# A hybrid attention and HGRN2 block: the second weight pair as four blocks instead of seven products

## The reference

```
proj = h @ w_in                       # (1024, 1024) @ (1024, 10240)
sb_q, sb_k, sb_v, sb_z, hg_q, hg_f, hg_i, hg_z, gate_logits = split(proj)
w[i, j] = sigmoid(z_ij) * prod_{j < l < i} (1 - sigmoid(z_il)),  z = q k^T / sqrt(128)   # stick-breaking, 8 heads
f = lb + (1 - lb) sigmoid(hg_f);  S_t = f S_{t-1} + (1 - f) v_t^T;  o_t = S_t^T silu(hg_q)   # HGRN2, 8 heads
y = sigmoid(gates_sb) * (sb_o * silu(sb_z)) @ w_sb + sigmoid(gates_hg) * (norm(hg_o) * silu(hg_z)) @ w_hg
out = rmsnorm(x + y @ w_out) * final_norm_g
```

## Time and profile before

| what | us |
|---|---|
| median of 3 runs | 1380.04 (1379.36 to 1381.21) |
| the profiled execution | 1382.87 |
| its span | 1381.1 |
| TensorE busy | 1340.9 (97%) |
| VectorE busy | 944.4 (68%) |
| GpSimd busy | 724.6 (52%) |
| ScalarE busy | 585.0 (42%) |

### The profile page before, as it was taken

The page is one execution under the profiler, slowest core; times in us unless marked ns, Lnnn a source line. Parts: engine busy times, 40 slices in busy tenths (PEclk is TensorE's granted clock), DMA queues, the critical chain, the costliest instruction groups (busy, mean ns, idle before and its releaser), DMA issues.

```text
span 1381.1 us, 23094 instructions
## 1 busy us (share of the span) xinstructions
PE 1340.9 (97%) x8421; PEld 1115.3 (81%) x8421; DVE 944.4 (68%) x1075; ACT 585.0 (42%) x965; POOL 724.6 (52%) x484
## 2 busy tenths in 40 slices
PE   7989999999999999999999999999999989999998
PEld 6778788788888878878878888887877868788886
DVE  5868877877967987787796797888544634545323
ACT  7645356256346435625634633653444411101121
POOL 5965554744665556565466456554678622223210
PEclk9989999999999999999999999999999999999999
DMA  5111311121112211121111211115452475433502
GB/s 184 31 46 31 93 61 32 63 77 46 63 31 67 63 56 61 32 90 64 31 63 59 64 63 32 62 40 145 167 192 98 143 238 191 134 92 122 199 26 103
DMA packets 128221, 119.41 MB, mean 86 GB/s; under 512 B 3920, under 2 KB 110464, under 8 KB 128128
## 3 DMA queue, kind: packets, MB, share of 16 engines
q1 hardware_dynamic: 118912, 92.84, 21.2%
q10 hardware_dynamic: 9216, 25.17, 5.2%
HBM read 88.63 MB, written 29.36 MB: 85 GB/s over the span
## 4 chain that ended last, share of the span: by engine, by line
PE 83%; DVE 5%; POOL 3%; issue 2%; ACT 1%; DMA 1%; DVEq 0%; ACTq 0%; POOLq 0%
PE banks L1695 46%; PE banks L2005 11%; PE banks L2027 6%; PE banks L1780 5%; PE banks L1756 4%; PE banks L1770 2%; POOL b_lo L638 1%; PE banks L1839 1%; POOL b_sum L638 1%; DVE hk L1176 1%; PE banks L1814 1%; PE banks L1739 1%; PE banks L1841 1%; PE banks L1834 1%; PE banks L1820 1%
## 5 line engine op out<-in xcount | busy, mean ns | idle before, releaser
L1695 PE MATMUL banks<-a_hi,b_hi 128*128 128x512 f32 x1092 | 444.5, 407 | 9.0 <-DVE k_raw L1176 4.3
L1695 PE MATMUL banks<-a_hi,b_lo 128*128 128x512 f32 x1092 | 428.5, 392 | 0.0
L1695 PE MATMUL banks<-a_lo,b_hi 128*128 128x512 f32 x1092 | 427.4, 391 | 0.0
L638 POOL TENSOR_TENSOR b_lo<-w_raw,b_hi 128x512 fp32r<-128x512 f32 x106 | 162.2, 1540 | 222.6 <-ACT b_hi L747 222.6
L638 POOL TENSOR_TENSOR b_lo<-b_sum,b_hi 128x512 fp32r<-128x512 f32 x117 | 176.0, 1504 | 156.0 <-ACT b_hi L747 156.0
L1695 PEld LDWEIGHTS banks<-a_hi,b_hi 128*128 128x128 f32 x1092 | 205.9, 189 | 51.3 <-issue 6.8
L1695 PEld LDWEIGHTS banks<-a_hi,b_lo 128*128 128x128 f32 x1092 | 205.7, 188 | 45.5
L1695 PEld LDWEIGHTS banks<-a_lo,b_hi 128*128 128x128 f32 x1092 | 206.4, 189 | 37.1
L1307 DVE TENSOR_TENSOR_SCAN kappa<-kappa 128x128 f32<-128x128 f32 (+3 forms) x64 | 90.9, 1421 | 86.6 <-ACT kappa L924 86.6
L747 ACT ACTIVATE b_hi<-b_sum 128x512 fp32r<-128x512 f32 x117 | 73.9, 632 | 156.1 <-POOL b_sum L638 151.2
L731 POOL TENSOR_TENSOR w_lo<-w_raw,w_hi 128x1024 fp32r<-128x1024 f32 x20 | 54.9, 2747 | 143.8 <-ACT w_hi L747 143.8
(11 more groups left out here) (218 smaller groups left out, 2584.5 us busy)
## 6 DMA issues: line engine op xcount, KB each, us to landing
w_raw<-in_w_in SPq DMA_DIRECT2D x72, 512.0 KB, 5.0
gate_d<-gate_out SPq DMA_DIRECT2D x16, 512.0 KB, 3.3
gate_in<-gate_d ACTq DMA_DIRECT2D x32, 256.0 KB, 2.7
x_tok<-in_x SPq DMA_DIRECT2D x8, 512.0 KB, 5.7
z_d<-z_out SPq DMA_DIRECT2D x8, 512.0 KB, 2.6
hz_d<-z_out SPq DMA_DIRECT2D x8, 512.0 KB, 2.6
osb_d<-o_sb SPq DMA_DIRECT2D x8, 512.0 KB, 7.1
ohg_d<-hq SPq DMA_DIRECT2D x8, 512.0 KB, 2.7
```

The lines of the kernel that those rows point to most:

```text
L638: return nc.gpsimd.tensor_tensor(dst, a, b, op)
L1695: last = mm(bank, w[:, s, k, :], t[s][:, k, :], start=opens and k == 0 and z == 0, stop=k == QUAD - 1 and z == 2, skip_group_check=not opens)
```

## The change

The second pair is done like the first, in four blocks of (token half, panel): (1, 0), (1, 1), (0, 0), (0, 1), into banks 4 to 7. Its weights are split without sums, in places named by `second_weights`, one of them the first pair's. GpSimd makes four low halves in place of seven and three sums. ScalarE copies the finished blocks to `turn_in` and `z_out` (`take_second`), between the splits of the third pair; VectorE's sums over them are gone, and so are `c12_step` and its wait. VectorE makes the low halves of k and q before those of P5 and P3. The high half of P3 now waits for two blocks of the second pair. TensorE waits for `block_taken` 5 and for all four sums of h (`s_ready` 4) after the second pair. SyncE loads the third pair after the second's last low half. `sum_t7` of the third pair raises `raw_sum` by 9, so that later counts agree. The small rows are fetched by ScalarE's queue ahead of `norm_tiles`. `fetch_gate(0)` stands before the last `finish_gate` and its waits.

```diff
-SECOND_ORDER = (P1, P2, P4, P7, P6, P5, P3)
-SECOND_BANKS = {P1: 4, P2: 5, P4: 6, P7: 7, P6: 2, P5: 4, P3: 3}
+SECOND_BLOCKS = {(1, 0): 4, (1, 1): 5, (0, 0): 6, (0, 1): 7}
+FIRST_SUM = 9
...
     if isinstance(n, int) and n == 1:
-        return PRODUCTS + SECOND_ORDER.index(s) + 1
+        return {P2: PRODUCTS + 3, P3: PRODUCTS + 3, P4: 2 * PRODUCTS, P6: PRODUCTS}.get(s, 1)
...
+        def second_weights(rows, panel):
+            s = {(0, 0): P2, (1, 0): P3, (0, 1): P4}.get((rows, panel))
+            return first_b[0, 0] if s is None else (b_hi[:, s, :, :], b_lo[:, s, :, :])
...
@@ sync, load_pair and the first loads @@
                 elif isinstance(n, int) and n == 2:
-                    sp.wait_ge(raw_sum, 4 * n)
-                    sp.wait_ge(w_ready, PRODUCTS + SECOND_SPLIT_ORDER.index(P3) + 1)
+                    sp.wait_ge(w_ready, 2 * PRODUCTS)
...
             load_x(1)
-            load_small(0, KT, norm_g[0].rearrange("(k p) -> k p", p=P))
...
             load_x(2)
@@ gpsimd @@
             pool.wait_ge(w_loaded, 32)
-            second_split(P1, raw_block(0, 0))
-            second_split(P2, raw_block(1, 0))
-            tt(part_of(b_sum, P5), raw_block(0, 1), raw_block(0, 0), ALU.subtract).then_inc(raw_sum, 5)
...
+            for i, (rows, panel) in enumerate(FIRST_BLOCKS[:3]):
+                second_low(rows, panel, i + 1)
             pool.wait_ge(a_ready, KT)
             tt(flat(raw_a12), flat(a_hi[P2]).bitcast(F32), flat(a_lo[P2]).bitcast(F32), ALU.add).then_inc(a_back, 1)
-            second_split(P4, part_of(b_sum, P4))
-            second_split(P7, part_of(b_sum, P7))
             pool.wait_ge(first_rows_done, 1)
-            second_split(P6, t2_flat)
-            second_split(P5, part_of(b_sum, P5))
+            second_low(*FIRST_BLOCKS[3], 4)
@@ scalar @@
+            load_small(0, KT, norm_g[0].rearrange("(k p) -> k p", p=P))
...
             norm_tiles(0, 4)
...
             sum_high(P7, raw_s3, s3_made)
-            split_second(P4)
+            split_second(3)
             sum_high(P6, raw_s2, s2_made)
-            for s in (P7, P6, P5):
-                split_second(s)
             sum_high(P5, raw_s1, s1_made)
             take_first(1, 3)
             take_first(3, PRODUCTS)
-            sum_high(P3, raw_s4, s4_made)
-            act.wait_ge(product_done, products_before(1, P1))
-            copy(u3[:, :], banks[:, SECOND_BANKS[P1], :]).then_inc(p1_copied, 2)
...
             copy(k_hi[:, :], first_out[:, 2:4, :].rearrange("p a n -> p (a n)")).then_inc(k_hi_ready, 1)
-            split(2, SPLIT_ORDER[0])
             copy(q_hi[:, :], first_out[:, 0:2, :].rearrange("p a n -> p (a n)")).then_inc(q_hi_ready, 1)
+            for t in SPLIT_ORDER[:2]:
+                split(2, t)
...
+            def take_second(tokens, panel, done):
+                act.wait_ge(product_done, PRODUCTS + done)
+                return copy(halfs((turn_in, z_out)[panel], tokens), banks[:, SECOND_BLOCKS[tokens, panel], :])
+            take_second(1, 0, 1).then_inc(p1_copied, 2)
+            act.wait_ge(qk_split, 2)
+            take_second(1, 1, 2).then_inc(block_taken, 5)
+            sum_high(P3, raw_s4, s4_made)
             act.wait_ge(lb_step, 1)
             nc.scalar.activation(lb[:, :], lb_low, ACT.Sigmoid).then_inc(lb_step, 1)
-            for t in SPLIT_ORDER[2:-1]:
+            for t in SPLIT_ORDER[2:4]:
                 split(2, t)
+            take_second(0, 0, 3).then_inc(first_taken, 2)
+            for t in SPLIT_ORDER[4:-1]:
+                split(2, t)
+            take_second(0, 1, PRODUCTS).then_inc(block_taken, 5)
...
-            finish_gate(N_GATE_PAIRS - 1)
-            for i in range(2):
-                act.wait_ge(gate_stored[i], 16 * N_GATE_PAIRS)
+            fetch_gate(0)
+            finish_gate(N_GATE_PAIRS - 1)
+            for i in range(2):
+                act.wait_ge(gate_stored[i], 16 * N_GATE_PAIRS)
             act.wait_ge(product_done, PRODUCTS * N_PAIRS)
             fetch_ohg(0)
-            fetch_gate(0)
             fetch_ohg(1)
@@ vector @@
             low_sum(P6, raw_s2, 2)
+            dve.wait_ge(k_hi_ready, 1)
+            tt(k_lo[:, :], first_out[:, 2:4, :]..., k_hi[:, :].bitcast(F32), ALU.subtract).then_inc(qk_split, 1)
+            dve.wait_ge(q_hi_ready, 1)
+            tt(q_lo[:, :], first_out[:, 0:2, :]..., q_hi[:, :].bitcast(F32), ALU.subtract).then_inc(qk_split, 1)
             low_sum(P5, raw_s1, 3)
             low_sum(P3, raw_s4, 4)
...
-            second_done(P2)
-            tt(halfs(turn_in, 0), second_bank(P2), u3[:, :], ALU.add).then_inc(first_taken, 1)
...
-            tt(u2[:, :], second_bank(P5), u2[:, :], ALU.add).then_inc(c12_step, 1)
...
@@ tensor @@
-                    if isinstance(h, int) and h == 0:
-                        pe.wait_ge(c12_step, 1)
...
-            for s in SECOND_ORDER:
-                second_product(s)
+            for i, ((tokens, panel), bank) in enumerate(SECOND_BLOCKS.items()):
+                if i == 0:
+                    pe.wait_ge(w_ready, PRODUCTS + 2)
+                    pe.wait_ge(s3_made, QUAD)
+                if i == 1:
+                    pe.wait_ge(w_ready, 2 * PRODUCTS)
+                if i == 2:
+                    pe.wait_ge(s1_made, QUAD)
+                for k in range(KT):
+                    last = first_block(tokens, panel, k, second_weights, bank)
+                last.then_inc(product_done, 1 if i < 3 else 4)
+            pe.wait_ge(block_taken, 5)
+            pe.wait_ge(s_ready, 4)
             pe.wait_ge(const_made, CONSTANTS)
```

More of the change, by code:

```diff
@@ L646, in sum_t7 @@
             def sum_t7(n, raw=w_raw):
-                tt(part_of(b_sum, P7), raw_block(0, 1, raw), raw_block(1, 1, raw), ALU.subtract).then_inc(raw_sum, 1)
+                tt(part_of(b_sum, P7), raw_block(0, 1, raw), raw_block(1, 1, raw), ALU.subtract).then_inc(
+                    raw_sum, FIRST_SUM if isinstance(n, int) and n == 2 else 1)
             def sum_t5(n, raw=w_raw):
@@ L677, in _, with second_low @@
                 tt(raw_a11[:, k, :], a_hi[P1][:, k, :].bitcast(F32), a_lo[P1][:, k, :].bitcast(F32), ALU.add).then_inc(a_back, 1)
-            def second_split(s, raw):
-                split(1, SECOND_SPLIT_ORDER, s, raw)
-            pool.wait_ge(w_loaded, 32)
-            second_split(P1, raw_block(0, 0))
-            second_split(P2, raw_block(1, 0))
-            tt(part_of(b_sum, P5), raw_block(0, 1), raw_block(0, 0), ALU.subtract).then_inc(raw_sum, 5)
[L687 to L692, removed]
+            def second_low(rows, panel, made):
+                pool.wait_ge(hi_ready, PRODUCTS + made)
+                hi, lo = second_weights(rows, panel)
+                tt(lo.rearrange("p k e -> p (k e)"), raw_block(rows, panel), hi.rearrange("p k e -> p (k e)").bitcast(F32),
+                   ALU.subtract).then_inc(w_ready, 1 if made < 4 else 4)
+            pool.wait_ge(w_loaded, 32)
+            for i, (rows, panel) in enumerate(FIRST_BLOCKS[:3]):
+                second_low(rows, panel, i + 1)
             pool.wait_ge(a_ready, KT)
             tt(flat(raw_a12), flat(a_hi[P2]).bitcast(F32), flat(a_lo[P2]).bitcast(F32), ALU.add).then_inc(a_back, 1)
-            second_split(P4, part_of(b_sum, P4))
-            second_split(P7, part_of(b_sum, P7))
             pool.wait_ge(first_rows_done, 1)
-            second_split(P6, t2_flat)
-            second_split(P5, part_of(b_sum, P5))
+            second_low(*FIRST_BLOCKS[3], 4)
             def prepare(n, raw=w_raw, loaded=w_loaded, count=None):
@@ L774, in split_first, with split_second @@
                 copy(first_weights(rows, panel)[0].rearrange("p k e -> p (k e)"), raw_block(rows, panel)).then_inc(hi_ready, 1 if i < 3 else 4)
[L776 to L781, removed]
+            def split_second(i):
+                rows, panel = FIRST_BLOCKS[i]
+                act.wait_ge(w_loaded, 32)
+                if i == 3:
                     act.wait_ge(first_rows_done, 1)
-                copy(part_of(b_hi, s), raw_operand(s)).then_inc(hi_ready, 1)
+                copy(second_weights(rows, panel)[0].rearrange("p k e -> p (k e)"), raw_block(rows, panel)).then_inc(hi_ready, 1 if i < 3 else 4)
             def split(n, s, raw=w_raw, loaded=w_loaded, count=None):
@@ L812, in sum_high, with load_small @@
                 if s == P3:
-                    act.wait_ge(product_done, PRODUCTS)
+                    act.wait_ge(product_done, PRODUCTS + 2)
                 copy(flat(a_hi[s]), flat(raw)).then_inc(s_hi_ready, 1)
+            def load_small(row, n, src):
+                act.dma_start(small_rows[row:row + n, :], src).then_inc(small_in, 16)
+            load_small(0, KT, norm_g[0].rearrange("(k p) -> k p", p=P))
+            load_small(KT, KT, lb_logits[0])
+            load_small(2 * KT, KT, lb_logits[1])
+            load_small(3 * KT, KT, hg_norm_g[0])
+            load_small(4 * KT, 2 * KT, b_gate[0].rearrange("(k p) -> k p", p=P))
             norm_tiles(0, 4)
```

(34 more changed lines are left out.)

18 lines of the change are left out of this document (removed).

## The result

The kernel after takes 1383.89 us (median of 20 runs, 1380.36 to 1389.01), the kernel before in the same runs 1380.39 (20 runs, 1378.5 to 1384.12). The ratio is 1.0028, 95% interval 1.0019 to 1.0038. The forecast was 1370.5 with a range of 1366.8 to 1375.0: wrong in sign, and 13 us off. The profiled execution of after took 1384.1 (span 1382.4).

The account below looks back on a forecast made before the run. TensorE, busy 97% of the span, was taken as the bound. Gains of 8.0 (second pair), 0 (small rows) and 2.0 (gate) made 10.0 us, taken as 9.5: 1370.5 us, range 1366.8 to 1375.

Parts of the forecast that it names:

- What bounds the kernel: TensorE is busy 97%; only two waits, 8.0 and 5.8 us, count, and the stretch between moves as a whole.
- Second pair and the next wait: At the second and third pairs, TensorE's 8.0 us wait shrinks to 0.4; first turn of `beta` 8.0 us sooner.
- B: Rival: GpSimd and VectorE alternate at 3.34 us, TensorE waits at `turn_values` and first turn; 1373.1 us, chance 0.20.
- my own schedule: GpSimd's third-pair operations timed one by one, with t4 and the low halves done by 72.8 us.
- Small rows: At the start, moving the small rows to ScalarE's queue gains 0; bounds 1.7 us gained, 0.5 lost.
- the limit I gave: Sign of small rows landing late on the second queue: their transpose on TensorE comes later than 12 us.
- Gate: Before the tail's second panel, the 5.8 us wait becomes 3.9, released by GpSimd's `w_lo`; 2.0 us gained.
- E: Rival: block (0,1) is copied late behind slow GpSimd operations, so TensorE stalls at `turn_values`; 1388.5 us, chance 0.03.
- the six: The listed outcomes: terms as summed, new wait, late small rows, more than summed, slower, old wait not ended.

Follow-up runs that it names:

- the part alone, without the stops: Kernel before with only the second and third pairs' part of the change, plus 24 spare TensorE instructions before its loop: 1369.63 us, ratio 0.9928.
- an experiment of its own: Kernel before with only the five small rows moved to ScalarE's queue: 1379.51 us, ratio 0.9996.
- gate_only: Kernel before with only the first gate's request moved ahead of the last finish_gate: 1377.74 us, ratio 0.9981.
- after_w48: Kernel after with 24 more TensorE instructions (48 satisfied waits) before its loop over heads: 1367.45 us, ratio 0.99.
- after_w256: Kernel after with 128 more TensorE instructions (256 satisfied waits) before its loop: 1381.47 us in a single run.
- after_w512: Kernel after with 256 more TensorE instructions (512 satisfied waits) before its loop: 1407.04 us in a single run.
- after_hint: Kernel after, unpadded, with TensorE's loop written with the language's hint for the branch back: 1367.73 us, ratio 0.9915.
- after_w8: Kernel after with 4 more TensorE instructions (8 satisfied waits) before its loop: 1387.19 us in a single run.

## Why the prediction was wrong

**What bounds the kernel: the step that failed.** I wrote: "Everything between is a long dense stretch that I take to move as a whole: its loops wait on their own steps, none on a clock time". It did not move as a whole. The stretch is also a stream of instructions whose place changed with the change, and that cost 14.5 us: 11.1 at six heads and 3.4 of half clock. I counted the 12 added matmuls at their time on the array and not at their 24 instructions. Without the stops the forecast would have stood 3 us too high, in its range: 1367.45 against 1370.5 (1366.8 to 1375.0).

**Second pair and the next wait: right in kind, small in size.** Forecast 8.0 us (4.9 to 8.5); the part alone, without the stops, gave 9.9, above my upper bound, though its interval (8.0 to 11.7) reaches below that bound. In the two profiled executions `beta` is 10.2 sooner, of which 1.36 is there before the second pair begins (42.90 against 44.26) and is no gain of the change: half clock at the start lasted to 21.3 in before's profiled execution and to 18.5 in after's. The faster matmuls of the pair (0.2267 for 0.2325) are another 0.56 of the forecast's gap.

**B, alternation at 3.34 throughout: not so.** t4 ended at 70.7, 2.1 us before my own schedule, and `turn_values` never waited.

**Small rows: right**, at 0, by an experiment of its own. Their transpose came at 11.93 where 12 was the limit I gave.

**Gate: right in kind, small in size.** 2.0 forecast (1.0 to 4.5), 2.7 measured; the wait that replaced the old one is the one named, 4.28 in after, 3.4 in gate_only and 3.3 to 4.5 in the other versions, 3.9 forecast.

**Rivals.** E, the slower case, was a stall of TensorE at `turn_values`; there is none (no entry for L1720 in the waits). None of the six was about the instruction stream. Two things in before could have warned me: its 0.18 us without a releaser at 251.21, 3.2 us behind the loop's head, and its 79 packets of instructions, more than a program of one pass needs (26 in after_w48). The Trainium skill, "Runtime: NRT & Kernel Launch", "Instruction fetch mechanics", says that an engine's instructions come in blocks of 256, that crossing into the next is mostly hidden, and that a taken branch out of the window that is held forces a fetch. The runs agree on the blocks (16 KB packets; after_w256 and after_w512) and on the fetch after a branch; what they add is that the crossing behind a branch is hidden only by the work ahead of it. For how much is held the section gives two figures, 2048 instructions for TensorE (eight blocks) and a window of two blocks. The window of two is not what these runs show: in after_w48 a body of 1722 instructions, 6.7 blocks, is branched back over in 0.2 us. The eight blocks fit all runs, as follows.

**Why 24 instructions make the body stay while 128 don't.** In after the stop is eight instructions behind the head, so the head is at place 248 of its block of 256, and 248 + 1722 reaches into an eighth block; so does before's at 229, and so does the head with 128 more, at 120 (1842). With 24 more it is at place 16, and 16 + 1722 = 1738 fits in seven (1792). The times of the packets say what else is held. In after the eleventh packet comes at 222.4, ahead of the first branch back at 233.1, and each branch back is followed by nine packets: the body's eight blocks and one fetched ahead. In after_w48 the eleventh comes too, at 223.2, and then none until 928.3, behind the loop: seven blocks and the one ahead stay. In after_hint the head is at 248 and the body (1723 records with the hint) has its eight blocks, and yet it stays: only ten packets come ahead of its first branch, and the eleventh at 911.6, behind the last. So eight blocks held, the one fetched ahead among them, fit every run here, and the hint spared the one ahead. That is read from six places of the head (16, 120, 229, 239, 248, 252) and one hint; no run varied the body's size.

## What to carry to other kernels

An edit ahead of a loop on the engine that is the bound moves the whole loop in its instruction blocks, and here 19 instructions cost 10 us of 1380 with no other change. Before believing that an edit lost, look at the same place of each iteration for idle time without a releaser, look at the packets of the instruction queue, and time the edit once more with the loop's hint on its branch back, or a few dozen spare instructions ahead of it; price the parts of a change only with the loop at one alignment.

## What the runs showed of the hardware

- A branch back on TensorE takes 3.3 to 3.9 us, or 0.2 when the body is kept; the long one cost nothing here, with 14 to 17 matmuls already handed over.
- The next block is fetched only when the branch is over: at 24 stops TensorE went on 2.99 to 3.62 us behind the branch's end, 2.8 to 3.4 us behind the head's first matmul at the four first heads shown.
- Of the six stops in after, the two longest (2.09 and 2.00 us) were followed by half clock for 3.4 us, the four of 1.58 to 1.89 were not. Length alone does not decide it: in after_w8 stops of 2.05 and 2.08 us (at 587.1 and 819.2) were followed by half clock, and others of 2.08, 2.27, 2.28 and 2.36 were not.
- A satisfied semaphore wait costs TensorE some 0.1 us an instruction when it is not covered: 23.82 - 10.01 = 13.8 us for 128 instructions.
- VectorE's 2048-column subtraction is 2.28 us alone and 3.38 beside GpSimd, whose operation is 1.3 alone and 3.3 beside it, so the slowing is mutual.
